# First attention group scored in blocks of 128 neighbouring queries against 256 keys

## The chip, the cores and the metric

The kernel runs on one core of one Trainium2 chip. The metric is the device time of one execution, in microseconds (us), as the median of several runs.

## What is computed

An encoder layer is applied to two groups of 512 tokens (width 1024) with the same weights: RMSNorm, then a mixer (retention with 4 heads, and three groups of dilated windowed attention with 8 heads of width 64 each, gated and merged), then an expert-choice MoE with 16 experts, and a final norm. The part that the change touches is attention. For head h, each group g gives an unnormalised sum, a maximum and a sum of exponentials, and the three are merged as one softmax:

```
ATT_GROUPS = ((128, 1), (512, 4), (2048, 16))      # (window, dilation)
band = |key - query| <= window // (2 * dil)        # within each residue class modulo dil
m = max(s);  p = exp(s - m);  l = sum(p);  acc = p @ v          # per group
w = exp(m_all - max over groups(m_all))
att = sum(w * acc) / sum(w * l)
```

So in the first group a query looks at the 64 tokens before and the 64 behind it; the second group looks at each fourth token within 256, the third at each sixteenth.

## The kernel before

**Layout.** The 512 tokens of a group (b = 0, 1) are kept by residue: a tile r of 128 tokens holds tokens 4q + r, q = 0..127. Products are made in parts: an operand is split into a rounded float32r part (`_hi`, by ScalarE) and the rest (`_lo`, by VectorE or GpSimd), and three float32r products (hi hi, hi lo, lo hi) are summed. Two attention heads share a tile, in halves of 64 rows (a = 0, 1), so one pass handles a pair of heads in all three groups; four passes (h) for each b. The PSUM buffers ps_proj, ps_tr, ps_sc and ps_out have two slots each.

**Order of work.** The order is written out by hand as a list of words that all engines follow, each in its own queue (`head_schedule`, `attention_schedule`, `column_schedule`). Waits are on counters (semaphores); an engine's queue is strictly in order. A pass is a head part and an attention part, 12 projection tiles P(u, i) each:

- Head part: P(0, i) are retention queries and keys (256 columns wide), P(1, i) and P(2, i) the halves of retention values and gates (512 columns, `project_values`, L902). Between them stand the scores and probabilities of the attention pair whose q, k, v the pass before has made.
- Attention part: P(g, i) are q, k, v of group g of the next pair (384 columns, L925), and beside them the last transposes, the value products V and the retention of this head (K, O, A).

**Steps of one head pair before**, for each residue tile r = 0..3. *S r* (L1021): scores of the first group, 128 queries of residue r against all 512 keys, as 3 products x 2 heads, each 64 rows deep and 512 columns wide; VectorE adds the mask and takes the maximum (L1933). *D r* (L1034): scores of groups two and three, float32, 2 groups x 2 heads, 128 keys each; VectorE the same (L1945), then the shared shift (L1953). ScalarE takes one exponential over 768 columns for each head with its sum (L1437); VectorE divides (L1896, L1897) into `prob[a]`. *T r* (in `transposes`, L986): 4 transposes of 128 x 128 for each head, copied by ScalarE to `prob_t` (L1447). *U r*: 4 more for groups two and three, copied by VectorE (L1966). *V* (L1054, L1059): values times probabilities, float32: for the first group 4 residue tiles x 2 heads with 512 query columns each, for the others 2 groups x 4 tiles x 2 heads with 128 columns. Other words: R (L986, L1005) transposes rotated queries and keys; W splits a piece of the next weight unit, first part by ScalarE (`split_unit`, L1380), rest by GpSimd in the head part (L741) and by VectorE in the attention part (L1854). In the list, the last step of a pair (T 3, U 3, V) falls into the attention part, or for the fourth pair into the first output column.

**Weights** come by SyncE: `load_unit` waits until one of two buffers `w_raw` has been split, and issues one DMA; `load_retention(h)` loads the q/k unit (w_a[h, 0]) and the two halves of the value and gate unit (L594), and `load_attention(h + 1)` three units for the next pair. While V is outstanding, the new values of the first group are put into `v_next` by ScalarE and copied to `v_a[0]` afterwards (L1459).

The counts of matmuls in the chain rows below are instructions; a float32 product shows as two, a float32r product or a transpose as one.

## Time and profile before

| | us |
|---|---|
| median of 3 runs | 2489.22 (2488.55 to 2489.57) |
| span of the profiled execution | 2486.3 |
| TensorE matmuls busy | 2460.4 (99%) |
| VectorE busy | 1648.8 (66%) |
| ScalarE busy | 1385.6 (56%) |
| GpSimd busy | 323.1 (13%) |

The span is cut in two: token mixing of both groups up to about 1360 us, then the experts. Times in the rows are microseconds from the start of the span unless marked ns. In the chain, each piece is a stretch of the work that ended last, with the number of instructions in it. PE is TensorE's matmul side, DVE VectorE, ACT ScalarE, POOL GpSimd, SPq the queue of SyncE's DMA issues. L12 is line 12 of the kernel.

### The profile page before, as it was taken

Reading aid. Unit: us, or ns where it says so; the run is one execution under the profiler, and the core shown is the slowest. Engines: PE = TensorE matmul, PEld = TensorE weight load, DVE = VectorE, ACT = ScalarE, POOL = GpSimd, SP = SyncE. Lnnn points to the kernel's source line nnn. Section 1 sums busy time; section 2 is a strip of 40 time slices with the busy share of each in tenths; the row PEclk is TensorE's granted clock in tenths of the full one; section 3 lists DMA queues with packets and bytes.
Section 4 is the critical chain, followed back from the end, with each engine's and each line's share of the span. In section 5 each row is a group of like instructions: output and inputs, shape, how many; then the busy total and the mean of one; then the engine's idle time right before and its main releaser. Section 6 shows DMA issues by size and latency. Waiting matters only on the chain.

```text
span 2486.3 us, 36774 instructions
## 1 busy us (share of the span) xinstructions
PE 2460.4 (99%) x12848; PEld 2096.6 (84%) x12848; DVE 1648.8 (66%) x2070; ACT 1385.6 (56%) x1542; POOL 323.1 (13%) x287
## 2 busy tenths in 40 slices
PE   8999999999999999999999999999999999999998
PEld 7898989788898989897887688888888888888886
DVE  5454545453544545554434788888888888888887
ACT  4434344432434444445333677777777777777776
POOL 1313122100013122220001100000000000000000
PEclk9999999999999999999999999999999999999999
DMA  4212121122712121112234999999999999999998
GB/s 173 94 41 86 51 93 47 64 85 93 271 54 84 52 93 57 70 53 75 78 145 158 361 386 395 376 399 382 391 383 387 379 386 385 379 389 390 387 383 305
DMA packets 133489, 550.59 MB, mean 221 GB/s; under 512 B 9392, under 2 KB 10032, under 8 KB 125488
## 3 DMA queue, kind: packets, MB, share of 16 engines
q1 hardware_dynamic: 126368, 524.03, 55.4%
q0 software_dynamic: 7056, 25.69, 3.4%
q8 instruction: 40, 0.66, 0.1%
q14 instruction: 25, 0.20, 0.0%
HBM read 528.72 MB, written 20.97 MB: 221 GB/s over the span
## 4 chain that ended last, share of the span: by engine, by line
PE 98%; DVE 1%; DMA 0%; ACT 0%; issue 0%; POOL 0%; SPq 0%; DVEq 0%; ACTq 0%; POOLq 0%
PE bank L1260 42%; PE bank L925 20%; PE bank L970 12%; PE bank L902 7%; PE bank L945 4%; PE bank L986 3%; PE bank L1093 2%; PE bank L1306 2%; PE bank L1054 1%; PE bank L1021 1%; PE bank L1074 1%; PE bank L1034 1%; PE bank L1059 1%; PE bank L1151 1%; PE bank L1109 0%; PE bank L1005 0%
## 5 line engine op out<-in xcount | busy, mean ns | idle before, releaser
L2304 DVE TENSOR_TENSOR m_lo<-m_raw,m_hi 128x2048 fp32r<-128x2048 f32 x380 | 867.4, 2290 | 121.0 <-ACT m_hi L1717 117.6
L1717 ACT ACTIVATE m_hi<-m_raw 128x2048 fp32r<-128x2048 f32 x382 | 733.5, 1921 | 259.9 <-PE bank L1260 256.7
L925 PE MATMUL bank<-w_hi,h_hi 128*128 128x384 f32 (+1 forms) x1024 | 340.9, 333 | 1.7 <-DVE h_lo L2147 0.9
L925 PE MATMUL bank<-w_hi,h_lo 128*128 128x384 f32 (+1 forms) x1024 | 329.9, 322 | 0.0
L925 PE MATMUL bank<-w_lo,h_hi 128*128 128x384 f32 (+1 forms) x1024 | 329.5, 322 | 0.0
L1260 PE MATMUL bank<-m_hi,xs_hi 128*128 128x512 f32 x1032 | 321.0, 392 | 0.0
L1260 PE MATMUL bank<-m_hi,xs_lo 128*128 128x512 f32 x1032 | 317.9, 389 | 0.0
L1260 PE MATMUL bank<-m_lo,xs_hi 128*128 128x512 f32 x1032 | 317.8, 389 | 0.0
L1854 DVE TENSOR_TENSOR w_lo<-w_raw,w_hi 128x1152 fp32r<-128x1152 f32 (+4 forms) x110 | 140.9, 1282 | 212.5 <-ACT w_hi L1380 212.5
L1260 PEld LDWEIGHTS bank<-m_lo,xs_hi 128*128 128x128 f32 x1032 | 193.8, 188 | 40.4
L1260 PEld LDWEIGHTS bank<-m_hi,xs_lo 128*128 128x128 f32 x1032 | 193.8, 188 | 40.3
L1260 PEld LDWEIGHTS bank<-m_hi,xs_hi 128*128 128x128 f32 x1032 | 191.5, 188 | 38.2 <-DVE xs_lo L2326 0.2
L925 PEld LDWEIGHTS bank<-w_hi,h_hi 128*128 128x128 f32 x1024 | 193.1, 189 | 7.8 <-issue 3.7
L925 PEld LDWEIGHTS bank<-w_lo,h_hi 128*128 128x128 f32 x1024 | 193.5, 189 | 0.2
L925 PEld LDWEIGHTS bank<-w_hi,h_lo 128*128 128x128 f32 x1024 | 193.0, 189 | 0.0
L1380 ACT ACTIVATE w_hi<-w_raw 128x768 fp32r<-128x768 f32 (+4 forms) x182 | 179.5, 995 | 12.0 <-PE bank L970 11.8
L730 POOL TENSOR_TENSOR rot<-rot,rot 128x256 f32<-128x256 f32 x128 | 94.4, 738 | 539.1 <-DVE rot L1890 538.3
L1260 PE MATMUL bank<-m_hi,hid_hi 128*128 128x512 f32 x496 | 154.2, 392 | 0.0
L1260 PE MATMUL bank<-m_lo,hid_hi 128*128 128x512 f32 x496 | 152.7, 389 | 0.0
L1260 PE MATMUL bank<-m_hi,hid_lo 128*128 128x512 f32 x496 | 152.7, 389 | 0.0
L741 POOL TENSOR_TENSOR w_lo<-w_raw,w_hi 128x768 fp32r<-128x768 f32 (+2 forms) x72 | 132.4, 1844 | 145.1 <-ACT w_hi L1380 144.7
L1400 ACT ACTIVATE v_a<-bank 128x128 f32<-128x128 f32 x78 | 21.6, 277 | 214.2 <-DVE rot L1890 214.2
(257 smaller groups left out, 3829.9 us busy)
## 6 DMA issues: line engine op xcount, KB each, us to landing
m_raw<-in_w_exp_gate SPq DMA_DIRECT2D x128, 1024.0 KB, 9.3
m_raw<-in_w_exp_up SPq DMA_DIRECT2D x128, 1024.0 KB, 7.0
m_raw<-in_w_exp_down SPq DMA_DIRECT2D x128, 1024.0 KB, 7.6
w_raw<-in_w_b SPq DMA_DIRECT2D x22, 1536.0 KB, 6.7
w_raw<-in_w_a SPq DMA_DIRECT2D x24, 1024.0 KB, 5.1
w_raw<-in_w_c SPq DMA_DIRECT2D x24, 1024.0 KB, 4.7
w_raw<-in_w_d SPq DMA_DIRECT2D x8, 1024.0 KB, 6.0
xt<-in_x SPq DMA_DIRECT2D x8, 512.0 KB, 8.8
```

The costliest lines, as they stand in the source:

```text
L730: pool.tensor_tensor(rot1[turn.slot][:, :], rot1[turn.slot][:, :], rot2[turn.slot][:, :], ALU.add).then_inc(s_rope, 1)
L741: ins = pool.tensor_tensor(w_lo[w.slot][:, cols], w_raw[w.slot][:, cols], w_hi[w.slot][:, cols].bitcast(F32), ALU.subtract)
L902: last = pe.matmul(sums, a[:, k, natural(i)], v[:, c, :, :], start=k == n == 0, stop=k == KC - 1 and n == 2)
L925: last = pe.matmul(ps_proj[:, proj.slot, 0:cols], a[:, c, tokens], v[:, c, :], start=c == n == 0, stop=c == chunks - 1 and n == 2)
L945: last = pe.matmul(ps_proj[:, proj.slot, :], a[:, c, natural(i)], v, start=c == n == 0, stop=c == KC - 1 and n == 2)
L970: last = pe.matmul(ps_proj[:, tile.slot, :], v[:, c, natural(cc)], a[:, c, :], start=c == n == 0, stop=c == chunks - 1 and n == 2)
L986: last = pe.transpose(ps_tr[0:cols, tr.slot, rows * j:rows * (j + 1)], a, ident[0:rows, 0:rows])
L1260: mm = pe.matmul(ps[:, half, :], a[:, chunk + k, :], v[:, k, 512 * half:512 * (half + 1)], start=first and k == n == 0, stop=last and k == ...
L1380: act.activation(w_hi[w.slot][:, cols], w_raw[w.slot][:, cols], ACT.Copy)\
L1717: act.activation(m_hi[slot.slot][:, :, :], m_raw[raw.slot][:, :, :], ACT.Copy)\
L1854: ins = dve.tensor_tensor(w_lo[w.slot][:, cols], w_raw[w.slot][:, cols], w_hi[w.slot][:, cols].bitcast(F32), ALU.subtract)
L2304: dve.tensor_tensor(m_lo[slot.slot][:, :, :], m_raw[raw.slot][:, :, :], m_hi[slot.slot][:, :, :].bitcast(F32), ALU.subtract)\
```

## The change

- The first group's queries are stored by blocks: tile i holds the 128 neighbouring tokens 128 i .. 128 i + 127 (in the order residue, then position), `by_block`. Against them stand 256 keys that cover the window (`window_keys`: 64 positions of each residue, read in runs of 32 elements) instead of 512. Tiles of groups two and three are still by residue.
- S i and D i become one step S i: 6 products of 256 columns and the 4 of groups two and three into the other half of the same PSUM slot. The four steps come earlier in the head part, and probabilities of all four tiles are kept, in `near` (first group) and `wide` (the others).
- Rows of `near` and of `wide` are now different queries on the same partition. Each gets its own maximum and its own sum (4 exponentials of 256 columns for each step). After the fourth step, maxima and sums are exchanged: VectorE spreads them over 128 columns with a 0/1 pattern (`spread`), the new word *I* is one float32 product with the 0/1 matrix `same`, VectorE picks its own, ScalarE takes one small exponential, VectorE forms the factors and scales the 16 tiles of 256 columns (`share_step`).
- T i has 4 transposes and U r has 4; results go back into `near` and `wide`.
- V: the second and third group as before; the first group is 4 blocks x 2 key chunks x 2 heads of 128 columns. Its output is written to the residue order (`block_rows`: four runs of 32 columns, 128 apart).
- The values for the key chunks have to be on other partitions: SyncE writes `v_a[0]` to DRAM (256 KB), waits for it, and reads seven overlapping chunks back with four DMAs (`v_shifted`), each pass, between w_a[h, 0] and the next weights (`shift_values`). `v_next` and its copy go away.
- The mask table has the same size, with three window masks and the 0/1 matrix. At the start VectorE makes the pattern `group` from the identity, before it sets the constant `eps`.

The diff, cut to its core:

```diff
@@ -126,12 +129,12 @@
-    order = "P S0 P D0 P P T0 S1 P U0 D1 P P T1 S2 P U1 D2 P P T2 S3 P U2 D3 P"
+    order = "P S0 P P S1 P S2 P P S3 P P I P P T0 U0 P T1 U1 P T2 U2"
     tiles = [(u, i) for u in range(3) for i in range(NT)]
@@ -564,6 +585,22 @@
+        def block_rows(a, i):
+            return a.rearrange("p (r q) -> p r q", r=RES)[:, :, BLOCK * i:BLOCK * (i + 1)]
+        def by_block(a, r):
+            return a.rearrange("p (i r q) -> p r i q", i=NT, r=RES)[:, r, :, :]
+        def window_keys(k, i):
+            rows = k.rearrange("p (r q) -> p r q", r=RES)[:, :, window(i):window(i) + WIN]
+            return rows.rearrange("p r (c q) -> p c r q", c=2)
+        def window(i):
+            return min(max(BLOCK * i - BLOCK // 2, 0), P - WIN)
@@ -571,12 +608,19 @@
+        v_kept = nc.dram_tensor("v_kept", (P, RES, P), F32, kind="Internal").ap()
+        def kept_rows(r):
+            row = RES * P
+            return bass.AP(v_kept.tensor, r * P, [[row, BLOCK], [BLOCK // 2 * row, SHIFTED], [1, P]])
@@ -585,8 +629,24 @@
+            def shift_values():
+                all_read(sp, s_proj_free, t["proj"], but=2 * NT)
+                apart(sp, s_apart_sp)
+                sp.wait_ge(s_out, START + t["out"].n())
+                apart(sp, s_apart_sp)
+                sp.dma_start(v_kept, v_a[0][:, :, :]).then_inc(s_kept, 16)
+                sp.wait_ge(s_kept, t["swap"].n() * 16 + 16)
+                apart(sp, s_apart_sp)
+                for r in range(RES):
+                    sp.dma_start(v_shifted[BLOCK * r:BLOCK * (r + 1), :, :], kept_rows(r)).then_inc(s_shifted, 16)
+                t["swap"].k += 1
+                t["proj"].k += PER_HEAD["proj"]
+                t["out"].k += PER_HEAD["out"]
             def load_retention(h):
                 load_unit(w_a[h, 0], KC * NA)
+                shift_values()
                 for part in range(2):
@@ -1010,56 +1072,61 @@
                         all_read(pe, s_tr_free, tr, but=1)
                     all_read(pe, s_sc_free, sc)
                     q_hi, k_hi = qk_t[0][:, 0, :], qk_t[0][:, 1, :]
                     for n, (q, k) in enumerate(((q_hi, k_hi), (q_hi, k_lo), (q_lo, k_hi))):
                         for a in range(2):
-                            last = pe.matmul(ps_sc[:, a, :], q[head_rows(a), natural(r)], k[head_rows(a), :],
-                                             start=n == 0, stop=n == 2)
-                            if n == 2:
-                                last.then_inc(s_sc, 1)
-                                sc.k += 1
...
+                            pe.matmul(ps_sc[:, a, 0:2 * P], q[head_rows(a), natural(i)], window_keys(k[head_rows(a), :], i),
+                                      start=n == 0, stop=n == 2)
                     for g in (1, 2):
                         for a in range(2):
-                            last = pe.matmul(ps_sc[:, a, P * (g - 1):P * g], qk_t[g][head_rows(a), 0, natural(r)],
-                                             qk_t[g][head_rows(a), 1, natural(r)], start=True, stop=True)
+                            last = pe.matmul(ps_sc[:, a, P * (g + 1):P * (g + 2)], qk_t[g][head_rows(a), 0, natural(i)],
+                                             qk_t[g][head_rows(a), 1, natural(i)], start=True, stop=True)
                             if g == 2:
                                 last.then_inc(s_sc, 1)
                                 sc.k += 1
+                elif what == "I":
+                    pe.wait_ge(s_same, 1)
+                    all_read(pe, s_sc_free, sc)
+                    pe.wait_ge(s_spread, t["swap"].n(1))
+                    pe.matmul(ps_sc[:, 0, 0:P], same[:, :], spread.rearrange("p g k s c -> p (g k s c)"),
+                              start=True, stop=True).then_inc(s_swapped, 1)
+                    t["swap"].k += 1
                 elif what == "T":
-                    for a in range(2):
-                        pe.wait_ge(s_prob, step.n(1))
-                        transposes([prob[a][:, natural(j)] for j in range(4)])
-                        step.k += 1
+                    i = arg[0]
+                    pe.wait_ge(s_prob, step.n(1 + 2 * i))
+                    transposes([near[:, i, a, natural(c)] for a in range(2) for c in range(2)])
                 elif what == "U":
-                    transposes([prob[a][:, natural(j)] for a in range(2) for j in (4, 5)])
+                    r = arg[0]
+                    pe.wait_ge(s_prob, step.n(2 + 2 * r))
+                    transposes([wide[:, r, a, natural(g)] for a in range(2) for g in range(2)])
+                    if r == RES - 1:
+                        step.k += 2 * RES
                 elif what == "V":
                     all_read(pe, s_tr_free, tr)
                     all_read(pe, s_out_free, outs)
-                    for r in range(RES):
-                        for a in range(2):
-                            pe.matmul(ps_out[head_rows(a), a, :], v_a[0][:, r, head_rows(a)], prob_t[:, a, r, :],
-                                      start=r == 0, stop=False)
+                    pe.wait_ge(s_shifted, t["swap"].n() * 16 * RES)
                     for g in (1, 2):
                         for r in range(RES):
                             for a in range(2):
-                                last = pe.matmul(ps_out[head_rows(a), a, natural(r)], v_a[g][:, r, head_rows(a)],
-                                                 prob_t[:, a, RES + g - 1, natural(r)],
-                                                 start=False, stop=g == 2 and r == RES - 1)
-                                if g == 2 and r == RES - 1:
+                                pe.matmul(ps_out[head_rows(a), a, natural(r)], v_a[g][:, r, head_rows(a)],
+                                          wide[:, r, a, natural(g - 1)], start=g == 1 and r == 0, stop=False)
+                    for i in range(NT):
+                        for c in range(2):
+                            rows = window(i) // (BLOCK // 2) + 2 * c
+                            for a in range(2):
+                                last = pe.matmul(block_rows(ps_out[head_rows(a), a, :], i), v_shifted[:, rows, head_rows(a)],
+                                                 near[:, i, a, natural(c)], start=False, stop=i == NT - 1 and c == 1)
+                                if i == NT - 1 and c == 1:
@@ -1423,40 +1490,40 @@
-                        act.activation(qk_t[u][:, :, natural(i)],
-                                       ps_tr[:, tr.slot, 0:2 * P].rearrange("p (a n) -> p a n", a=2),
-                                       ACT.Copy).then_inc(s_tr_free[tr.slot] if u else s_pair_hi, 1)
+                        if u == 0:
+                            act.activation(by_block(qk_t[0][:, 0, :], i),
+                                           ps_tr[:, tr.slot, 0:P].rearrange("p (i q) -> p i q", i=NT), ACT.Copy)
+                            act.activation(qk_t[0][:, 1, natural(i)], ps_tr[:, tr.slot, P:2 * P], ACT.Copy)\
+                                .then_inc(s_pair_hi, 1)
...
-                        act.wait_ge(s_sm, START + score.n(1))
-                        act.activation(prob[a][:, :], prob[a][:, :], ACT.Exp, bias=shift[:, a:a + 1],
-                                       scale=DH ** -0.5, accum_out=psum_row[:, a:a + 1]).then_inc(s_exp, 1)
-                        score.k += 1
+                    act.wait_ge(s_sm, START + score.n(1))
+                    for side, scores in enumerate((near, wide)):
+                        for a in range(2):
+                            last = act.activation(scores[:, i, a, :], scores[:, i, a, :], ACT.Exp,
+                                                  bias=stats[:, 0, 0, side, i, a:a + 1], scale=DH ** -0.5,
+                                                  accum_out=stats[:, 0, 1, side, i, a:a + 1])
+                    last.then_inc(s_exp, 1)
+                    score.k += 1
+                elif what == "I":
+                    t["swap"].k += 1
+                    act.wait_ge(s_gap, t["swap"].n())
@@ -1581,15 +1648,17 @@
+                            if (u, i) == (0, 0):
+                                act.wait_ge(s_shifted, t["swap"].n() * 16 * RES)
+                            if (u, i) == (1 if tail else 0, 0):
                                 act.wait_ge(s_out, START + outs.n())
                             if kind == "open" and b > 0 and i == 0:
                                 stored(b, (1,) if u < 2 else (), u == 2)
                             act.wait_ge(s_rope_x, t["turn"].n())
-                            dst = v_next[:, i, :] if tail and u == 0 and i < NT - 1 else v_a[u][:, i, :]
-                            projected(dst, ps_proj[:, proj.slot, 2 * P:3 * P])
+                            projected(v_a[u][:, i, :], ps_proj[:, proj.slot, 2 * P:3 * P])
                         elif u == 0:
@@ -1890,13 +1960,39 @@
-            def scale_step(a):
-                dve.wait_ge(s_exp, t["step"].n(1))
-                then(dve.reciprocal(pinv[:, a:a + 1], psum_row[:, a:a + 1]))
-                dve.tensor_scalar(prob[a][:, :], prob[a][:, :], pinv[:, a:a + 1], None, ALU.mult)\
-                    .then_inc(s_prob, 1)
-                t["step"].k += 1
+            def share_step():
+                dve.wait_ge(s_exp, t["score"].n())
+                for side in range(2):
+                    own = stats[:, 0, :, 1 - side, :, :].rearrange("p k i a -> p k (i a)")
+                    last = dve.tensor_tensor(spread[:, :, :, side, :], own.unsqueeze(1).to_broadcast([P, NT, 2, 8]),
+                                             group[:, :].unsqueeze(2).unsqueeze(3).to_broadcast([P, NT, 2, 8]), ALU.mult)
+                last.then_inc(s_spread, 1)
+                t["swap"].k += 1
+                dve.wait_ge(s_swapped, t["swap"].n())
+                then(dve.tensor_tensor(picked.rearrange("p (m i a) -> p m i a", i=NT, a=2),
+                                       ps_sc[:, 0, 0:P].rearrange("p (m i a) -> p m i a", i=NT, a=2),
+                                       group[:, :].unsqueeze(1).unsqueeze(3).to_broadcast([P, 16, NT, 2]), ALU.mult))
+                then(dve.tensor_reduce(stats[:, 1, :, :, :, :].rearrange("p k s g a -> p g (k s) a"),
+                                       picked.rearrange("p (g m i a) -> p g m a i", g=NT, i=NT, a=2), AXX, ALU.add))
+                lows = stats[:, :, 0, :, :, :].rearrange("p w s g a -> p w (s g a)")
+                sums = stats[:, :, 1, :, :, :].rearrange("p w s g a -> p w (s g a)")
+                then(dve.tensor_tensor(least[:, :], lows[:, 0, :], lows[:, 1, :], ALU.min))
+                dve.tensor_tensor(gap[:, :, :], least[:, :].unsqueeze(1).to_broadcast([P, 2, 16]), lows,
+                                  ALU.subtract).then_inc(s_gap, 1)
+                dve.wait_ge(s_share, t["swap"].n())
+                then(dve.tensor_tensor(gap[:, :, :], share[:, :, :], sums, ALU.mult))
+                then(dve.tensor_tensor(total[:, :], gap[:, 0, :], gap[:, 1, :], ALU.add))
+                then(dve.reciprocal(total[:, :], total[:, :]))
+                then(dve.tensor_tensor(factor[:, :, :, :].rearrange("p s g a -> p (s g a)"), share[:, 0, :], total[:, :],
+                                       ALU.mult))
+                for i in range(NT):
+                    for side, scores in enumerate((near, wide)):
+                        for a in range(2):
+                            last = dve.tensor_scalar(scores[:, i, a, :], scores[:, i, a, :],
+                                                     factor[:, side, i, a:a + 1], None, ALU.mult)
+                        last.then_inc(s_prob, 1)
@@ -1915,56 +2011,45 @@
+                    i = arg[0]
+                    if i == 0:
+                        dve.wait_ge(s_out, START + outs.n())
                     dve.wait_ge(s_sm, START + score.n())
-                    r = arg[0]
                     for a in range(2):
                         dve.wait_ge(s_sc, sc.n(1))
                         apart(dve, s_apart_dve)
+                        at = 2 * P * ((0, 1, 1, 2)[i])
                         dve.tensor_tensor_reduce(
-                            out=prob[a][:, 0:T], in0=ps_sc[:, sc.slot, :],
-                            in1=mask0[:, P * (3 - r):P * (3 - r) + T], scale=1.0, scalar=-3.0e38,
-                            op0=ALU.add, op1=ALU.max, accum_out=top[:, 2 * a:2 * a + 1])\
+                            out=near[:, i, a, :], in0=ps_sc[:, sc.slot, 0:2 * P], in1=mask0[:, at:at + 2 * P],
+                            scale=1.0, scalar=-3.0e38, op0=ALU.add, op1=ALU.max, accum_out=top[:, i, 0, a:a + 1])
+                        dve.tensor_tensor_reduce(
+                            out=wide[:, i, a, :], in0=ps_sc[:, sc.slot, 2 * P:4 * P], in1=mask12[:, :],
+                            scale=1.0, scalar=-3.0e38, op0=ALU.add, op1=ALU.max, accum_out=top[:, i, 1, a:a + 1])\
                             .then_inc(s_sc_free[sc.slot], 1)
                         sc.k += 1
@@ -2150,6 +2235,8 @@
+            dve.wait_ge(s_ident, 16)
+            then(dve.reduce_sum(group[:, :], ident[:, :].rearrange("p (g q) -> p g q", g=NT), AXX))
             then(dve.memset(aff_pad[0][:, :], 0.0))
```

## Rows read from the trace of the kernel before

**Rows 1.** The page: busy time, share, instructions; the chain by engine.
```profile
PE 2460.4 (99%) x12848; PEld 2096.6 (84%) x12848; DVE 1648.8 (66%) x2070; ACT 1385.6 (56%) x1542; POOL 323.1 (13%) x287
...
PE 98%; DVE 1%; DMA 0%; ACT 0%; issue 0%; POOL 0%; SPq 0%; DVEq 0%; ACTq 0%; POOLq 0%
```

**Rows 2.** TensorE's waits, whole run, the first row: total us, times, longest.
```profile
PE bank L1109 <- DMA ident<-in_ident: 5.0, 1, 5.0
```

**Rows 3.** Busy time in one head stretch: engines, granted clock, DMA share, GB/s.
```profile
186.42:236.80 50.38, 50.38 (x319) 42.59 (x319) 24.13 (x78) 23.90 (x43) 20.66 (x14) 1.00 0.27 101
```

**Rows 4.** Chain in order of time, head part: start, us, line, instructions.
```profile
186.42 2.88 PE bank L925 x24
...
189.51 0.89 PE bank L1021 x4
...
193.69 0.65 PE bank L1034 x8
...
200.71 0.87 PE bank L986 x8
...
205.65 0.44 PE bank L986 x4
...
206.73 5.67 PE bank L902 x24
```

**Rows 5.** The same view, attention part: value products; transposes after O3.
```profile
131.73 3.58 PE bank L1054 x16
135.31 1.75 PE bank L1059 x32
...
172.12 0.22 PE bank L986 x2
```

**Rows 6.** TensorE's timeline around one step S: start, duration.
```profile
189.44 0.50 PE L1021 MATMUL bank<-qk_t 64*128 64x512 f32 x2
189.78 0.39 PE L1021 MATMUL bank<-k_lo,qk_t 64*128 64x512 f32 x2
190.01 0.39 PE L1021 MATMUL bank<-qk_t,q_lo 64*128 64x512 f32 x2
190.34 0.39 PE L925 MATMUL bank<-w_hi,h_hi 128*128 128x256 f32 x1
```

**Rows 7.** Groups by line and shape up to 1160 us: busy, mean ns.
```profile
L986 PE MATMUL bank<-ident,prob 128*128 128x128 f32 x384 | 52.3, 272 | 0.0
```

**Rows 8.** VectorE's timeline: four scalings, and a masked maximum.
```profile
175.00 1.14 DVE L2012 TENSOR_SCALAR v_g<-v_g,small 128x256 f32<-128x256 f32 x4 [1.07 <-ACT small L1481]
...
194.89 0.41 DVE L1945 CUSTOM_DVE_ANT_0 prob<-bank,mask 128x256 f32<-128x256 f32 x1
```

**Rows 9.** ScalarE's timeline: squares with sums, splits of weights.
```profile
172.59 0.37 ACT L1476 ACTIVATE bank<-bank 128x256 f32<-128x256 f32 x1 [1.36 <-DVE v_g L2003]
...
172.96 0.38 ACT L1476 ACTIVATE bank<-bank 128x256 f32<-128x256 f32 x1
...
187.35 0.84 ACT L1380 ACTIVATE w_hi<-w_raw 128x768 fp32r<-128x768 f32 x1
...
197.55 0.62 ACT L1380 ACTIVATE w_hi<-w_raw 128x512 fp32r<-128x512 f32 x1
```

**Rows 10.** GpSimd's timeline: the last piece of a unit.
```profile
200.00 1.29 POOL L741 TENSOR_TENSOR w_lo<-w_raw,w_hi 128x512 fp32r<-128x512 f32 x1
```

**Rows 11.** SyncE's DMA issues in order of time.
```profile
134.87 0.33 SPq L585 DMA_DIRECT2D w_raw<-in_w_a  x1
162.67 21.28 SPq L594 DMA_DIRECT2D w_raw<-in_w_a  x2
```

**Rows 12.** DMA issues, whole run: KB each, median us to landing.
```profile
w_raw<-in_w_a SPq DMA_DIRECT2D x24, 1024.0 KB, 5.1
...
normed<-norm POOLq DMA_DIRECT2D x8, 512.0 KB, 2.9
```

**Rows 13.** VectorE's timeline at the start of the span.
```profile
8.14 0.16 DVE L2042 RECIPROCAL small<-small 128x1 f32<-128x1 f32 x1 [6.87 <-DMA gain_row<-in_gain_rows]
```

160 lines of the change are left out of this document (82 added, 78 removed).

## The prediction

> **What bounds the kernel now.** I read the page first: TensorE is busy 99% of the span and the chain that ended last is 98% TensorE [rows 1]. The reader is to see that no other engine carries the end: what TensorE issues is the time. Second, TensorE's waits over the whole run: the longest of all is the 5.0 us for the identity at the very start [rows 2], and asked for the stretch of one head, 186.4 to 237 us, that view lists none; TensorE's busy time there equals the stretch [rows 3]. The granted clock there is 1.00, so the upper of the two levels, 2.4 GHz, while VectorE and ScalarE are each busy under half of it [rows 3]. TensorE never pauses there and I see no reason for the clock to fall afterwards. So a matmul taken out of this stretch shortens the kernel by its spacing in the chain, and a new wait counts in full. Third, the chain in order of time, which gives the spacing of each step (not the latency of one matmul, which is longer since they overlap) [rows 4, 5]. There are 8 such passes (4 head pairs in each of 2 token groups) and 4 steps i in each, 32 steps in all.
>
> **Scores (S and D).** Before, a step is 6 float32r matmuls of 512 columns, 0.89 us, and 4 float32 products of 128 columns, which show as 8 instructions, 0.65 us [rows 4]: 1.54 us. After, the 6 have 256 columns and the 8 follow at once. In detail the three pairs start 0.34, 0.23 and 0.33 us apart [rows 6]; the middle one is the bare pair, the outer two hold about 0.1 us each of changing between 128-row and 64-row operands. What do 256 columns less give? Tiles of 24 matmuls take 2.88 us at 256 columns and 12 take 5.67 / 2 us at 512 [rows 4]: 0.120 and 0.236 us each, so 0.116 less. Three pairs: 0.35. One changeover (S to a projection) is gone since D follows directly: 0.10. But the weight loads set a floor: D's eight come at 0.08 us each [rows 4], so a pair can't go below 0.16 and six are at least 0.48. I take 0.50 + 0.65 = 1.15, a saving of 0.39 per step, 32 x 0.39 = 12.5 us. Bounds: if the two heads no longer overlapped, six at 0.120 are 0.72, a saving of 0.17 or 5.4 us; with the full 0.45, 14.4 us. The moving operand is now read in runs of 32 elements; no row shows what that costs, and I take nothing, since a run is 128 bytes long; the low bound covers it.
>
> **Transposes (T and U).** 12 per step before (384 in 32 steps [rows 7]), 0.87 + 0.44 = 1.31 us [rows 4]; 8 after, at the same 0.109 each: 0.87. Saved 32 x 0.44 = 14.0 us. The form is unchanged; the bounds are 13.5 and 14.1.
>
> **Values (V).** 8 products of 512 columns take 3.58 us, 16 of 128 take 1.75 us [rows 5]. After, the first kind is replaced by 16 more of 128 columns (4 blocks x 2 key chunks x 2 heads). By the row of the second kind they take 1.75: saved 1.83 per pass, 8 x 1.83 = 14.6 us. The stationary operand has the same shape as there, and the two heads still use different column halves. New is that the output is written in four runs of 32 columns, 128 apart. All rows of the trace write in one run, so no row prices this; the lower end is 0 extra, the upper end is that each run costs what a 128-column product costs now: 4 x 1.75 - 1.75 = 5.25 us per pass, 42 us. I take 0, because L1059 costs a quarter of L1054 per product (0.109 and 0.448): the spacing goes by columns, and nothing is paid for a new place in the output.
> The Trainium skill speaks against this: "PSUM — Partial Sum Buffer", Specifications (TRN2), says that any non-contiguous access pattern there slows matmuls significantly. It gives no factor; it is the slow-output rival below.
>
> **Exchange (I).** One float32 product of 128 x 128, two instructions. Two transposes take 0.22 us [rows 5]; with two changeovers 0.45. I take 0.30: 8 x 0.30 = +2.4 us, bounds 1.8 and 3.6.
>
> **Does the exchange come in time?** The wait sits in TensorE's queue at I, and projection P(2,0) and all behind it are queued there. Counted from S3's end at about 23.6 us into the head: VectorE starts 0.3 later and runs four masked maxima of 256 columns at 0.35 to 0.41 us (0.41 by its duration [rows 8], 0.35 by its share of a 512-column one) and a small operation of 0.2: 25.5. ScalarE's four exponentials with sums: squares of the same shape come 0.37 apart [rows 9]: 27.1. VectorE's two multiplies of 64 elements, 0.25 each by my estimate (the smallest operation takes 0.16 [rows 13], one of 256 columns 0.41): 27.7. TensorE reaches I after two value tiles, 5.7 us [rows 4]: 29.4. Margin 1.7 us. After I, VectorE needs 4 short operations (1.1), ScalarE 0.25, VectorE 4 more (0.8), and the first two scalings at 0.285 each [rows 8]: 29.8 + 2.7 = 32.5, while T0 comes two tiles later at 35.4. Margin 2.9. All 16 scalings end at 36.8; U0's copy waits behind them on VectorE, and its buffer is wanted by U1 at 39.6. S2 follows S1 by only one tile and a transpose, 3.1 us, and needs S1's four maxima read: 1.8. Margin 1.3. Each costs nothing.
>
> **What the exponentials push back.** ScalarE's splits of the weights share its queue, and GpSimd makes the rest of each after it. The last piece of the second value unit stands behind S3's exponentials: ScalarE 27.2 to 27.8 (0.62 [rows 9]), GpSimd 1.29 more [rows 10]: 29.2. P(2,0) wants it at 29.75. This margin, 0.5 us, is the thinnest one. I take 0.1 us per pass for it, 0.7 us; bounds 0 and 0.5 per pass (4 us).
>
> **SyncE.** It now stands still after load w_a[h,0] (issued 134.87 [rows 11]) until the last retention output O3 (172.1 [rows 5]), one write of 256 KB and its landing, and issues four reads ahead of the next weights. Before, those weights were issued at 162.67 and landed about 5.1 later [rows 11, 12]. A 512 KB write lands in 2.9 us [rows 12], so 172.1 + 3 + four issues of 0.4 = 177, + 5.1 and about 1.5 for the reads' own bytes = 183.5. Their first user is ScalarE at 187.35 [rows 9]. Margin 3.9 us: cost nothing. If it were gone, ScalarE's queue would stop, then rotations and scores with it, and TensorE would pay the excess in each pass. The second half of that unit has its buffer free only at the end of the 21.28 us that the row spans, near 184 [rows 11], so it and all behind it don't move.
>
> **At nothing:** VectorE now waits for the identity before the small constant is set, so ScalarE's first square slips from 4.8 to about 6; VectorE's first use waits for the gain row until 8.14 anyway [rows 13]. The query halves copied by ScalarE in two instructions instead of one, and v_a written without the later copy, lie under 4.2 us tiles. In the expert stage too no wait of TensorE exceeds those 5.0 us [rows 2], so it just starts earlier.
>
> **Sum.** 12.5 + 14.0 + 14.6 - 2.4 - 0.7 = 38.0 us. Profiled span 2486.3 - 38.0 = 2448.3; the runs' median 2489.22 lies 2.9 above that span, so 2451.2; I say 2451. With all low bounds but the slow output (5.4 + 13.5 + 14.3 - 3.6 - 4 = 25.6) it is 2463.6; with all high ones (14.4 + 14.1 + 14.8 - 1.8 = 41.5) 2447.7.
>
> **Rivals.**
> (a) Scores don't shrink with their columns: loads or short runs set the spacing. For: D's row is already load-bound, 128 columns at 0.08 us. Against: L1021's middle pair is 0.23. It gives the 7.1 us between 12.5 and 5.4 back: 2458. The Trainium skill's "TensorE: Matmul & The Clock Gate", LDWEIGHTS, puts 128 weight columns at 107 ns whatever the rows; six are then 0.64 and by that estimate the saving is 8.3 us, the time 2455. The trace has them faster in pairs, 0.08.
> (b) The exchange or the splits end late: three queues in a row, each a little slower than I have it, 1 to 2.5 us per pass exposed, 8 to 20 us back: 2459 to 2471. For: a 0.5 us margin. Against: VectorE and ScalarE were busy under half of the stretch.
> (c) Slow output, ending on the other side. Place: V's 16 block products. It decides against the change when they take 1.75 + 38.0 / 8 = 6.5 us per pass, 3.7 times the contiguous ones. At four times (each run as a full product) it is 2451 + 42 = 2493. A factor of 2 would give 2451 + 14 = 2465. For: nothing in the trace, which has no such output. Against: spacing in L1059 goes by columns alone. The Trainium skill's PSUM rule above speaks for it.
> (d) The pieces are less dense than the matmuls removed, and TensorE gives more than the sum: under 2447.
>
> **Chances.** Forecast with its own spread 2446 to 2457: 0.64. (a) 0.11, (b) 0.10, (c) at twice 0.07, (c) at about four times 0.05, (d) 0.03. The range 2446 to 2468 leaves out (d), the far end of (b) and the slow side of (c). A measurement of this kernel can tell about 0.2% (5 us) from no change. Faster 0.93, same 0.02, slower 0.05.
>
> **What would show it.** In the profile after: masked windows' matmuls 0.48 to 0.55 us per step; 256 transposes of probabilities in 32 steps, not 384; V as two stretches of 1.75 us; I at 0.3 with no wait ahead of it or of P(2,0). TensorE's list of waits should still hold only the start and the seams. A row of TensorE waiting for w_lo of GpSimd, for the spread statistics or for the scaled probabilities would make (b) right; a V stretch well over 3.5 us makes (c) right.

## The result and the profile after

The changed kernel takes 2441.53 us (median, 2441.01 to 2443.08) against 2488.89 us beside it: a ratio of 0.9814, 95% interval 0.98 to 0.9828, 47 us less. The direction was as forecast. The size was not: 38 us were forecast, and 2441.5 lies under the range of 2446 to 2468. The profiled execution spans 2439.9 us, 46.4 less than before.

The page after, the rows that answer to [rows 1]: busy time and the chain by engine.

```profile
PE 2412.3 (99%) x12864; PEld 2083.9 (85%) x12864; DVE 1623.7 (67%) x2119; ACT 1371.8 (56%) x1673; POOL 333.9 (14%) x287
...
PE 96%; DVE 2%; ACT 1%; issue 1%; POOL 0%; DMA 0%; DVEq 0%; POOLq 0%; ACTq 0%; SPq 0%
```

TensorE is still the bound, but the chain now leaves it for 4% of the span, where before it was 2%: there is a wait in each pass. (The chain follows the work that TensorE waited for over some 6 us per pass; TensorE itself stands still for 0.2 of them.) TensorE's waits after name it (total us, times, longest), in answer to [rows 2]:

```profile
PE bank L1176 <- DMA ident<-in_ident: 4.9, 1, 4.9
...
PE bank L964 <- POOL w_lo L803: 1.7, 8, 0.2
```

Now the chain in order of time through one head part, in answer to [rows 4] (start, us, line, instructions). L1084 are the six first-group products of a step, L1088 the eight instructions of groups two and three, L1048 and L1067 transposes.

```profile
180.20 2.88 PE bank L987 x24
183.08 0.22 PE bank L1048 x2
183.30 0.56 PE bank L1084 x3
183.85 0.45 PE bank L1088 x7
184.30 3.07 PE bank L987 x24
...
187.58 2.87 PE bank L987 x24
...
199.12 2.77 PE bank L964 x12
201.89 0.56 PE bank L1084 x6
202.45 0.50 PE bank L1088 x8
...
207.65 1.28 POOL w_lo L803
...
208.98 5.78 PE bank L964 x24
...
222.89 4.19 PE bank L987 x24
```

Read two things here. The eight instructions of groups two and three take 0.45 us where they took 0.65, though they are the same eight (some records are missing, so a row can show seven or three). And the tile behind a step takes 3.07 us, the tile behind a transpose 2.87: 0.2 us of "changing over" are booked on the projection that follows, not on the step. Before, both S and D paid both, as these tiles of the kernel before show, behind S, behind D, and behind a transpose:

```profile
190.40 3.07 PE bank L925 x24
...
194.33 3.06 PE bank L925 x24
...
197.61 2.88 PE bank L925 x24
```

I had looked only inside the steps.

The value products, in answer to [rows 5]:

```profile
127.20 1.95 PE bank L1121 x32
129.15 1.75 PE bank L1127 x32
```

The block products (L1127) take the 1.75 us that was forecast; the 0.2 us of entering this form, which L1054 carried before, now stand on L1121.

From the first to the second head part a pass took 115.07 us before (from 71.35 to 186.42 [rows 4]) and 109.31 after (70.89 to 180.20): 5.76 less, 8 x 5.76 = 46.1 of the 46.4 us. The head part (71.35 to 117.66 before, 70.89 to 113.56 after) went from 46.31 to 42.67 us in the first pass, the rest of the pass from 68.76 to 66.64. So nearly the whole difference is in the passes: per pass 3.6 us in the head part and 2.1 in the attention part.

### The profile page after: what moved, and what is told of

It is laid out like the page before. It is cut to its first block, busy times and chain, and to the rows that moved or that the text cites. A ratio compares the mean times of both kernels' runs of the same rounds, so it can differ in the third digit from the quotient of the medians.

```text
span 2439.9 us, 36720 instructions
## 1 busy us (share of the span) xinstructions
PE 2412.3 (99%) x12864; PEld 2083.9 (85%) x12864; DVE 1623.7 (67%) x2119; ACT 1371.8 (56%) x1673; POOL 333.9 (14%) x287
## 4 chain that ended last, share of the span: by engine, by line
PE 96%; DVE 2%; ACT 1%; issue 1%; POOL 0%; DMA 0%; DVEq 0%; POOLq 0%; ACTq 0%; SPq 0%
PE bank L1327 43%; PE bank L987 20%; PE bank L1032 13%; PE bank L964 6%; PE bank L1007 4%; PE bank L1048 3%; PE bank L1160 2%; PE bank L1373 2%; PE bank L1141 1%; PE bank L1084 1%; PE bank L1121 1%; PE bank L1088 1%; PE bank L1127 1%; PE bank L1218 1%; POOL w_lo L803 0%
## 5 line engine op out<-in xcount | busy, mean ns | idle before, releaser
L1467 ACT ACTIVATE v_a<-bank 128x128 f32<-128x128 f32 x96 | 26.7, 278 | 277.6 <-DVE rot L1960 277.6
L803 POOL TENSOR_TENSOR w_lo<-w_raw,w_hi 128x768 fp32r<-128x768 f32 (+2 forms) x72 | 142.8, 1996 | 106.1 <-ACT w_hi L1447 106.1
```

Source lines behind the costliest of these rows:

```text
L803: ins = pool.tensor_tensor(w_lo[w.slot][:, cols], w_raw[w.slot][:, cols], w_hi[w.slot][:, cols].bitcast(F32), ALU.subtract)
```

## The experiments

My theory after reading the two traces (A): a change of TensorE between 128-row operands and 64-row operands, in and out, costs about 0.39 us, and four per pass are gone. Rivals: the columns gave it (C), or a small price for a change and something else (B). Several kernels were timed side by side in a set; "the changed kernel" below is its run of the same set. The four runs from "Values written in one run" to "Without the exchange's product" have none beside them: they are compared by their ratio to the kernel before, 0.9814 for the changed kernel, and by their traces.

**The changed kernel again, as reference**

> The changed kernel itself, beside the others on the same chip: the reference point of this set. Both theories: 2441.5 us, 47 us under the kernel before, with a step of scores at 0.56 + 0.45 us, its exit into a 3.07 us tile (0.19 above 2.88), and TensorE waiting 0.2 us per pass for GpSimd's last piece.

Measured: 2442.78 us, ratio 0.9814 (0.9799 to 0.9829); TensorE waits 1.7 us in 8 times for GpSimd. As expected.

**Half the columns, in the kernel before**

```diff
-                            last = pe.matmul(ps_sc[:, a, :], q[head_rows(a), natural(r)], k[head_rows(a), :],
+                            last = pe.matmul(ps_sc[:, a, 0:2 * P], q[head_rows(a), natural(r)], k[head_rows(a), 0:2 * P],
...
-                            out=prob[a][:, 0:T], in0=ps_sc[:, sc.slot, :],
+                            out=prob[a][:, 0:T].rearrange("p (k n) -> p k n", k=2),
+                            in0=ps_sc[:, sc.slot, 0:2 * P].unsqueeze(1).to_broadcast([P, 2, 2 * P]),
```

> The kernel before with one part of the change alone: the six products of S take 256 key columns instead of 512. Part of the computation is left out (keys 256 to 511 of the first group get the scores of the first 256); S and D stay two steps apart, so the number of changes between 128-row and 64-row operands stays 8 per pass. Theory A (columns give 0.33 us per step, a pair of 256 columns at 0.12 us; the rest of the gain in scores is the four changes that the merged step avoids, some 0.39 us each): L1021 goes from 0.89 to 0.56, 32 x 0.33 = 10.6 us under the kernel before. Theory B (as predicted: a pair cannot go below 0.16 us for its weight loads, a change costs 0.1): 0.68 per step, 6.7 us under. Theory C (nearly all of the scores' gain of 22.6 us comes from the columns): 20 us or more under.

Measured: 2476.2 us against 2487.9, 11.7 less; ratio 0.9953 (0.9938 to 0.9968). The chain of this run:

```profile
187.54 0.55 PE bank L1021 x6
188.09 3.06 PE bank L925 x24
191.15 0.22 PE bank L1005 x2
191.36 0.65 PE bank L1034 x8
192.01 3.06 PE bank L925 x24
```

S is at 0.55 us, D still at 0.65, and both have a 3.06 us tile behind them. So columns give 0.34 us per step, 32 x 0.34 = 10.9 of the 11.7, which is A; the pair has no floor at 0.16 us, which was B. C is out: the scores gave about 23 us in all.

**The merged step cut in two, in the changed kernel**

```diff
+        if n + 1 < len(words) and words[n + 1] in ("S0", "S1", "S2"):
+            out.append(("s", int(words[n + 1][1])))
         if behind:
             out.append(behind.pop(0))
```

On TensorE the word s issues the six first-group products and S the other four; the other engines don't know s.

> The changed kernel with the merged step cut in two on TensorE: in steps 0, 1 and 2 the two 128-row transposes that stood ahead of the step now stand between its six first-group products and its four of groups two and three. Same instructions, same waits but for the order; 24 more changes from 64-row to 128-row operands and back. Theory A (a change out and in costs about 0.39 us): 24 x 0.39 = 9.4 us over the changed kernel. Theory B (0.1 us, as predicted): 2.4 us over. Theory C: nothing.

Measured: 2450.51 us against 2442.78, 7.7 more; the spans differ by 8.3 (2449.9 and 2441.6). One of its 24 places in the chain:

```profile
184.17 0.55 PE bank L1087 x6
184.72 0.37 PE bank L1051 x2
185.09 0.65 PE bank L1093 x8
185.74 3.08 PE bank L990 x24
```

The transposes between take 0.37 us instead of 0.22 (going out), and the eight instructions are back at 0.65 (coming in): 0.35 us per place, 24 x 0.35 = 8.4. A had 9.4, since going out into transposes costs 0.15 and into a projection 0.19; B had 2.4 and C nothing. With this run the price of a change is shown. What in the operands makes it a change is taken up in the part on why the prediction was wrong.

**The piece of weights ahead of the exponentials**

```diff
-        if i < len(PIECES):
+        if (u, i) != (1, 2) and i < len(PIECES):
             out.append(("W", i))
+        if (u, i) == (1, 1):
+            out.append(("W", 2))
```

> The changed kernel with the word W 2 of the second value unit moved ahead of S 3: ScalarE splits that piece while it waits for the statistics of S 3 and not behind the four exponentials. If the wait of P(2,0) is that piece alone (0.22 us per pass, 1.7 us in all, plus a slower first matmul after a stop, 0.1 us per pass): 1.7 to 2.5 us under the changed kernel and no wait of TensorE for GpSimd. If another wait stands right behind it (the exchange's product or a late unit): 0 to 0.5 us.

Measured: 2441.04 us against 2442.78, 1.7 less, but the ratios to the kernel before (0.9809 and 0.9814) have overlapping intervals, so the time alone doesn't settle it. The trace does: the wait for GpSimd is gone from the list, the head part takes 42.27 us (180.22 to 222.49) instead of 42.69, and the tile behind it has grown:

```profile
208.56 0.22 PE bank L1100 x2
208.78 5.50 PE bank L966 x24
...
221.53 0.87 PE bank L1050 x8
222.49 4.43 PE bank L989 x24
```

5.50 instead of 5.78 at P(2,0), but 4.43 instead of 4.19 at the first attention tile, and it starts 0.09 us after the transposes ahead of it end. So the wait at P(2,0) had cost 0.50 us per pass: 0.22 of standing still, and 0.28 in the tile behind it, whose first matmul without the stop starts 0.24 before the product ahead of it ends (208.54 and 208.78 in this run) and after a stop has nothing to overlap with. The head part got only 0.42 shorter, since 0.09 went into a new stop at its end. The exchange's product takes 0.22 us. The wait was real and its removal uncovered the next one.

**Values written in one run, and in single elements**

```diff
-                                last = pe.matmul(block_rows(ps_out[head_rows(a), a, :], i), v_shifted[:, rows, head_rows(a)],
+                                last = pe.matmul(ps_out[head_rows(a), a, natural(i)], v_shifted[:, rows, head_rows(a)],
```

> The changed kernel with the block products of V written in one run of 128 columns instead of four runs of 32 that lie 128 apart (the results land at the wrong queries, the work is the same). Theory A, from the profile after (1.75 us for the 16 products, as for contiguous ones): no difference, within 1 us of the changed kernel. The rule that any non-contiguous output slows a matmul: faster than the changed kernel by whatever it costs.

```diff
-                                last = pe.matmul(block_rows(ps_out[head_rows(a), a, :], i), v_shifted[:, rows, head_rows(a)],
+                                last = pe.matmul(ps_out[head_rows(a), a, :].rearrange("p (q r) -> p r q", r=RES)[:, i, :], v_shifted[:, rows, head_rows(a)],
```

> The changed kernel with the block products of V written in single elements, 4 apart, instead of runs of 32 (results land at the wrong queries, same work). If only the length of a run matters and 32 is long enough: the 16 products take clearly more than 1.75 us per pass, at twice 14 us and at four times 42 us over the changed kernel. If the output's pattern costs nothing at all: within 1 us.

Measured: 2441.14 and 2441.95 us, ratios 0.9813 and 0.9813 (0.9797 to 0.983 and 0.9796 to 0.9829). The matmuls of L1127 in the run with single elements (duration in ns, min, median, max):

```profile
L1127 PE MATMUL bank<-near,v_shifted x256: 272/273/273, 129.0 to 1112.4; 128*64 128x128 f32 x128
```

The changed kernel and the run with one run of 128 columns have the same 272 to 273 ns, and the chain has 1.75 us for the 32 instructions in all three. TensorE's output costs the same in one run of 128 columns, in four runs of 32 and in single elements 4 apart, for float32 products of 128 columns with 64 output partitions. Rival (c) is out. The Trainium skill's rule ("PSUM — Partial Sum Buffer", Specifications (TRN2)) that any non-contiguous access pattern slows matmuls significantly is not borne out for this form: 1.75 us each way. Float32r products and other engines' accesses were not tried.

**Keys read in one run**

```diff
-                            pe.matmul(ps_sc[:, a, 0:2 * P], q[head_rows(a), natural(i)], window_keys(k[head_rows(a), :], i),
+                            pe.matmul(ps_sc[:, a, 0:2 * P], q[head_rows(a), natural(i)], k[head_rows(a), 0:2 * P],
```

> The changed kernel with the moving operand of the six first-group products read as one run of 256 keys instead of runs of 32 (wrong keys, same work). Theory A, reading in runs of 128 bytes is free: L1084 stays at 0.56 us per step, within 1 us of the changed kernel. If runs cost something: under 0.56, for 0.05 us per step 1.6 us faster.

Measured: 2440.9 us, ratio 0.9809 (0.9792 to 0.9825). The two steps of one head part:

```profile
183.41 0.55 PE bank L1084 x6
...
190.78 0.54 PE bank L1084 x5
```

0.01 to 0.02 us less than 0.56, at most 0.6 us in all: too little to tell from the time.

**Without the exchange's product**

```diff
-                    pe.matmul(ps_sc[:, 0, 0:P], same[:, :], spread.rearrange("p g k s c -> p (g k s c)"),
-                              start=True, stop=True).then_inc(s_swapped, 1)
```

> The changed kernel without TensorE's product with the 0/1 matrix (statistics aren't exchanged, factors come from the row's own pattern): what the product costs by itself. Two 128-column instructions, 0.22 us per pass, and no other change since both neighbours are 128-row operands: 1.8 us under the changed kernel. But P(2,0) still waits for GpSimd's last piece, which ends at the same moment, so the wait grows by what the product gave: 0 to 0.5 us under. As predicted (0.30 per pass with nothing behind it): 2.4 us under.

Measured: 2441.44 us, ratio 0.9812. Its wait for GpSimd:

```profile
PE bank L964 <- POOL w_lo L803: 3.5, 8, 0.4
```

The wait grew from 1.7 to 3.5 us, by the 1.8 us that the product had taken. In the changed kernel the product is free, because P(2,0) would stand still anyway: of the two outcomes expected, the one with the wait behind it.

**A second reference**

> The changed kernel itself, the reference point of this set: 2441 to 2443 us, TensorE waiting 0.2 us per pass for GpSimd's last piece ahead of P(2,0).

Measured: 2441.75 us, ratio 0.9814 (0.9801 to 0.9827).

**Both pieces early**

```diff
             out.append((word[0], *map(int, word[1:])))
+            if word == "U0":
+                out.append(("W", 2))
             continue
...
-        if i < len(PIECES):
+        if (u, i) not in ((1, 2), (2, 2)) and i < len(PIECES):
```

> piece_early, and the last piece of the next unit (W 2 of the third) moved ahead of P(2,2) as well, behind U 0. In piece_early the gain at P(2,0), 0.42 us per pass in the head part, came back in part as a new wait of the first attention tile: it starts 0.09 us late and takes 4.43 us instead of 4.19, 0.3 us per pass, because GpSimd ends its third piece at the very moment. If that is all, GpSimd's pieces now follow without a gap and end 0.4 us earlier: 2.4 us under piece_early, 3 to 4 us under the changed kernel, and the tile is 4.19 again. If GpSimd's own pace is the bound (three pieces of the unit without a pause from the first on), the end doesn't move: 1 to 2 us under the changed kernel, as piece_early.

Measured: 2439.65 us against 2441.75, 2.1 less; ratio 0.9806 (0.9793 to 0.9819). The end did not move:

```profile
212.90 8.94 POOL L807 TENSOR_TENSOR w_lo<-w_raw,w_hi 128x1152 fp32r<-128x1152 f32 x3 [7.39 <-ACT w_hi L1451]
```

GpSimd works for 8.94 us without a pause, exactly as in piece_early, and the tile is still 4.45 us. My first expectation fell, the second (GpSimd's own pace) held.

**VectorE takes that piece**

```diff
+                            dve.wait_ge(s_whi, t["piece"].n(1))
+                            dve.tensor_tensor(w_lo[w.slot][:, cols], w_raw[w.slot][:, cols],
+                                              w_hi[w.slot][:, cols].bitcast(F32), ALU.subtract).then_inc(s_last, 1)
...
+                            pool.wait_ge(s_mid, t["swap"].n())
+                            pool.wait_ge(s_last, t["swap"].n())
+                            pool.sem_inc(s_wlo[w.slot], 1)
```

> both_pieces_early, and VectorE instead of GpSimd makes the rest of that last piece (0.96 us in VectorE's idle time behind U 0; GpSimd only signals when both are done). In both_pieces_early GpSimd works at the third unit without a pause, 8.94 us from 212.90 to 221.84, and the first attention tile takes 4.45 us and starts 0.09 late; GpSimd's own pace is then the bound. If so, this ends 2 us earlier, the tile is 4.19 again and nothing of TensorE's waits is left in the pass: 8 x 0.3 = 2.4 us less than both_pieces_early's 2439.65, 2437.3 us, a ratio to the kernel before of 0.9797. If the slow start of that tile has another cause: no change, 2439.7.

Measured: 2438.16 us (2437.3 to 2439.56), ratio 0.9803 (0.979 to 0.9816), against 2437.3 and 0.9797 expected.

```profile
208.32 5.50 PE bank L980 x24
...
221.94 4.19 PE bank L1003 x24
```

The tile is back at 4.19 and the head part at 42.18 us (179.76 to 221.94), 0.51 less than in the changed kernel, 4.1 us over the passes by the chain. By time it is 3.6 us below the changed kernel's second reference, from different sets, and the intervals of the ratios overlap: likely the fastest of all, and not shown to be so by times.

**SyncE held up longer**

```diff
-                sp.dma_start(v_kept, v_a[0][:, :, :]).then_inc(s_kept, 16)
-                sp.wait_ge(s_kept, t["swap"].n() * 16 + 16)
-                apart(sp, s_apart_sp)
+                for again in range(6):
+                    sp.dma_start(v_kept, v_a[0][:, :, :]).then_inc(s_kept, 16)
+                    sp.wait_ge(s_kept, t["swap"].n() * 96 + 16 * again + 16)
+                    apart(sp, s_apart_sp)
```

> The changed kernel with SyncE's write of the values to DRAM done and waited for six times instead of once, which holds the next weights back by five landings of some 2.1 us, 10.5 us. In the changed kernel they land near 175.4 and ScalarE first splits them at 181.1, a margin of 5.7. As predicted (an excess reaches TensorE through ScalarE's queue, in full): 4.8 us per pass, 38 us over the changed kernel. The rival: ScalarE is held up by 4.8 us, but what TensorE needs from it next (statistics of step 0 read, GpSimd's pieces before P(1,0) at 195.9) still comes in time, GpSimd ending near 194.3: within 2 us of the changed kernel.

Measured: 2460.24 us against 2441.75, 18.5 more. Neither: ScalarE's first split is 6.5 us late (187.65 instead of 181.13), and TensorE pays 18.5 / 8 = 2.3 per pass. Its waits:

```profile
PE bank L1068 <- POOL rot L793: 7.0, 5, 2.8
PE bank L965 <- POOL w_lo L804: 5.0, 8, 1.1
...
PE bank L965 <- DVE rqk_lo L2008: 2.2, 4, 0.7
PE bank L1085 <- DVE top L2036: 1.2, 4, 0.3
```

These four are 15.4 us, of the 21.6 by which this profiled execution is longer than the changed kernel's (2463.16 and 2441.56); 1.7 of them the changed kernel has as well, and the rest stands in no row of waits. They are uneven: at L1068 five passes wait, 0.2 to 2.8 us. What I had left out in "comes in time" is the transposes of rotated queries (L1068): GpSimd adds the rotation behind its piece, which waits for ScalarE.

## Why the prediction was wrong, point by point

**Scores: the step that failed.** I had 12.5 us, 0.39 per step. The columns gave 0.34 per step, 10.9 us, shown by the half-column run; my floor of 0.16 us per pair, read off D's eight instructions, was wrong. Those 0.65 us were 0.45 of work and 0.20 of coming in from 128-row operands, and I had taken it all for work. (My 0.236 us per 512-column matmul held a change too, since the 5.67 us tiles stand behind D; two such tiles behind a product of 128 rows take 5.50, 0.229 each, and the columns give 0.33 and not 0.35.) After that, TensorE's timeline in the changed kernel has the pairs 0.12 us apart, in answer to [rows 6]:

```profile
183.22 0.39 PE L1084 MATMUL bank<-qk_t 64*128 64x256 f32 x2
183.45 0.28 PE L1084 MATMUL bank<-k_lo,qk_t 64*128 64x256 f32 x2
183.57 0.28 PE L1084 MATMUL bank<-qk_t,q_lo 64*128 64x256 f32 x2
183.69 0.60 PE L1088 MATMUL bank<-qk_t 64*128 64x128 f32 x8
184.23 0.38 PE L987 MATMUL bank<-w_hi,h_hi 128*128 128x256 f32 x1
```

The term "one changeover is gone, 0.10" is the mis-sized one: its 0.10 and the floor together left 0.39 per step for columns and change, where 0.34 + 0.39 came. What is gone is a whole change, in and out, of 0.20 + 0.19 = 0.39 us per step: 32 x 0.39 = 12.5. Together 23.4 us instead of 12.5. The 0.19 was to be seen in the chain of the kernel before, between the rows of [rows 4]: its tiles of 24 matmuls take 3.07 us behind S and 3.06 behind D, and 2.88 elsewhere. I read the steps and did not compare the tiles next to them. Rival (d), a time under 2447, has the outcome; I gave it 0.03, and its reason, pieces "less dense", does not name the change. Rival (a) is out with the half-column run (its estimate of 8.3 us should have read 8.0, by its own 0.64).

Why a change costs that is only in part shown. Inside a projection tile the weight loads run ahead of their matmul; at the change they don't. After step 3 of the head part, the loads of the next tile:

```profile
202.82 0.19 PEld L964 LDWEIGHTS bank<-w_hi,h_hi 128*128 128x128 f32 x1
202.93 0.19 PEld L964 LDWEIGHTS bank<-w_lo,h_hi 128*128 128x128 f32 x1
203.16 0.19 PEld L964 LDWEIGHTS bank<-w_hi,h_lo 128*128 128x128 f32 x1
```

The first tile matmul starts at 202.82 too, so its load did not run ahead; the second and third start at 203.16 and 203.39, 0.23 after their loads. The Trainium skill's "TensorE: Matmul & The Clock Gate", The mechanism, says that a weight load is pulled ahead of matmuls in flight when it goes to a row group that they don't use, or to the background weight buffer. By the row groups alone the 128-row load behind 64-row matmuls would have to come late, as it does; but inside the projection tile loads of all 128 rows come 0.23 us ahead of their matmuls, while matmuls on the same rows are in flight. So the row groups alone don't tell when a load is early.

Nor are the 64 rows needed for the price. The value products use all 128 rows and only 64 output columns, and they pay the same: 1.95 us for the first 32 instructions and 1.75 for the next 32, so 0.20 going in, and the transposes behind them take 0.37 instead of 0.22, 0.15 coming out.

```profile
130.89 0.37 PE bank L1048 x2
```

The number format is not the reason either: the exchange's product is float32 between two float32r tiles, has all rows and columns, and takes 0.22 us, with nothing added. What S, D and V have in common is that a matmul uses one half of the rows or columns, in turn with the other half. Whether the half alone or the turns set the price was not tried, and so the cause of the 0.39 us stays open; its size and place are shown.

**Transposes.** 14.0 us forecast; 0.87 us per step for T and U together, 256 transposes instead of 384: right, 1.75 us per pass.

**Values.** 14.6 forecast, 5.33 - 3.70 = 1.63 per pass, 13.0 us, measured. The output pattern costs nothing, as chosen. Missed: the 0.2 us of entering belong to V whatever comes first, so they stood in the 3.58 of L1054 and were not saved with it.

**Exchange.** 2.4 us forecast; 0.22 us per pass or 1.8 measured, hidden by the wait behind it.

**The wait at P(2,0).** Foreseen as the thinnest margin, at 0.5 us, and put at 0.1 us per pass; it costs 0.50, as the run with the piece moved shows. By the sign that I had named, TensorE waiting for w_lo of GpSimd, rival (b) is there, at half its size or less. The step that was off most is ScalarE's four exponentials: I took 0.37 us each, from squares; they come 0.49 apart.

```profile
204.87 0.51 ACT L1509 ACTIVATE near<-near,stats 128x256 f32<-128x256 f32 x1 [2.91 <-DVE stats L2042]
...
205.38 0.49 ACT L1509 ACTIVATE near<-near,stats 128x256 f32<-128x256 f32 x1
```

4 x 0.12 = 0.5 us, the whole margin. The rest is that TensorE is at P(2,0) earlier than I had it, 5.81 us after S3 (202.95 to 208.76) and not 6.15. Cost: 8 x 0.50 = 4.0 us instead of 0.7. The kernel before had the better price, its own exponential, which reads a bias from a tile as the new ones do, where the squares do not:

```profile
195.69 0.94 ACT L1437 ACTIVATE prob<-prob,small 128x768 f32<-128x768 f32 x1 [0.28 <-DVE small L1953]
```

The splits of 768 and 512 columns, 0.84 and 0.62 [rows 9], give 0.22 us for 256 columns; taken off twice, 0.94 leaves 0.50, where 0.49 was measured. The first row of the changed kernel also shows ScalarE idle for 2.91 us ahead of them, which is where the moved piece fits.

**The sum again**, with what was measured: 10.9 + 12.5 + 14.0 + 13.0 - 1.8 - 4.0 = 44.6 us, for a span 46.4 us shorter. Of the 1.8 us between, 0.3 lie outside the passes; the rest, 0.2 per pass, I can't put down to a term. Against the forecast, scores gave 10.9 us more and the exchange cost 0.6 less, while values gave 1.6 less and the wait cost 3.3 more: the total was as near as it was because part of the error on the scores was taken back.

**The other margins** held. The exchange's product waited for nothing, S2 did not wait, T0 and U1 neither. SyncE wrote at 166.03 in the changed kernel and issued the next weights at 170.16; they take 5.2 us to land and are used at 181.13: 5.7 us of margin where I had 3.9. My statement on its loss was wrong in size: 6.5 us of lateness cost TensorE 2.3 per pass, not all of it. The later first square of ScalarE at the start moved nothing that can be seen: TensorE's first head part begins at 70.89 instead of 71.35, and the same kernel has 71.57 in another profiled execution.

## What to carry to other kernels

When TensorE is the bound, compare each kind of tile behind each kind of neighbour before pricing a step: here the change between operands of all 128 rows and columns and operands of half the rows or columns cost 0.35 to 0.39 us in and out, and stood partly on the step and partly on the tile behind it. Two short steps of the half kind that can stand together save that change, which here was worth more than halving the columns of one of them (12.5 and 10.9 us). Where a margin is thinner than the sum of small operations that fill it, price each by an operation of its own kind, with the same operands, and move what doesn't depend on the chain ahead of it: ScalarE's queue had 2.9 idle us right in front.

## What the runs showed of the hardware

- Changing from 128-row to 64-row operands costs TensorE 0.20 us (eight instructions in 0.65 instead of 0.45), changing back 0.19 into a projection (3.07 instead of 2.88) and 0.15 into transposes (0.37 instead of 0.22). Operands of 128 rows and 64 columns cost the same 0.20 going in (1.95 and 1.75) and 0.15 coming out (0.37 and 0.22).
- A stop of TensorE of 0.22 us costs 0.50: the tile behind it takes 5.78 us instead of 5.50.
- Pairs of 64-row matmuls on the two row halves come at 0.12 us for 256 columns, and the eight float32 instructions of 128 columns at 0.055 each.
- TensorE's output in runs of 32 columns or in single elements 4 apart costs no more than in one run: 272 to 273 ns each and 1.75 us for 32 in all three runs. Its moving operand in runs of 32 elements costs at most 0.02 us per six matmuls.
- An exponential of 128 x 256 with its sum and a bias from a tile takes 0.49 us of ScalarE, a square with its sum and no such bias, on PSUM, 0.37 [rows 9]. The function is not the reason as far as the trace before shows: its exponential of 896 columns without a bias takes 0.95 us, that of 768 columns with one 0.93.
- Seven overlapping chunks read back from DRAM with four DMAs of 112 KB land in 2.7 us (median), the 256 KB write before them in 2.0:

```profile
v_shifted<-v_kept SPq DMA_DIRECT2D x32, 112.0 KB, 2.7
...
v_kept<-v_a SPq DMA_DIRECT2D x8, 256.0 KB, 2.0
```
